# A two-block transformer on one core: an unused strip of 128 bytes in front of the split weights, and a ring of split rows that moves along

## What is computed

```
h @ w  ~  h_hi @ w_hi  +  h_lo @ w_hi  +  h_hi @ w_lo
```

## The kernel before, in words

| rows | distance before | distance after |
|---|---|---|
| HH, HLO, form A and B | 64 bytes | 192 bytes |
| ring HHR, HLR (16 numbers = 64 bytes on) | 0 | 0 |
| LATHI, LATLO (WHI is 73984 and 47104 bytes behind them) | 0 | 128 bytes |

## Time and profile before

### The profile page before, as it was taken

The page is one execution under the profiler, slowest core; times in us unless marked ns, Lnnn a source line. Parts: engine busy times, 40 slices in busy tenths (PEclk is TensorE's granted clock), DMA queues, the critical chain, the costliest instruction groups (busy, mean ns, idle before and its releaser), DMA issues.

```text
span 2110.5 us, 33942 instructions
## 1 busy us (share of the span) xinstructions
PE 2055.3 (97%) x13986; PEld 1863.4 (88%) x13986; DVE 1408.0 (67%) x2157; ACT 1009.3 (48%) x1492; POOL 131.8 (6%) x111
## 2 busy tenths in 40 slices
PE   5999999999999999999999999999999999999997
PEld 1678998788999999998888899999988999999986
DVE  2358999897677677666667576556676755566665
ACT  2234444645454444455445455444565544445553
POOL 0000000013000000000011011000010110000100
PEclk9999999999999999999999999999999999999998
DMA  9998798595777777656655546545555556545553
GB/s 362 383 358 309 240 381 324 197 355 165 236 246 237 233 231 249 196 169 244 190 177 207 176 153 201 197 141 169 164 186 180 174 151 220 168 155 164 177 191 120
DMA packets 267318, 462.98 MB, mean 219 GB/s; under 512 B 21526, under 2 KB 160028, under 8 KB 266652
## 3 DMA queue, kind: packets, MB, share of 16 engines
q1 hardware_dynamic: 265832, 459.66, 64.6%
q10 hardware_dynamic: 1332, 1.14, 0.2%
HBM read 458.62 MB, written 2.13 MB: 218 GB/s over the span
## 4 chain that ended last, share of the span: by engine, by line
PE 84%; DVE 7%; DMA 4%; issue 2%; ACT 2%; ACTq 1%; SPq 0%; POOL 0%; DVEq 0%
PE PS L315 36%; PE PS L314 19%; PE PS L1424 7%; PE PS L1434 7%; PE PS L1426 7%; DVE WLO L305 2%; PE PS L1266 2%; DMA AD<-w_ada 1%; DMA BIG<-w_ada 1%; DVE BIG L391 1%; DVE AD L391 1%; ACT WHI L297 1%; DMA X<-x 1%; PE PS L1280 1%; DVE BIG L1783 1%
## 5 line engine op out<-in xcount | busy, mean ns | idle before, releaser
L305 DVE TENSOR_TENSOR WLO<-RAWT,WHI 128x1024 fp32r<-128x1024 f32 (+7 forms) x694 | 833.0, 1206 | 392.5 <-ACT WHI L297 391.6
L297 ACT ACTIVATE WHI<-RAWT 128x1024 fp32r<-128x1024 f32 (+7 forms) x694 | 694.5, 1015 | 374.0 <-PE PS L1434 205.0
L315 PE MATMUL PS<-WHI,HH 128*128 128x512 f32 (+5 forms) x1296 | 502.6, 388 | 7.4 <-POOL HLO L1114 3.2
L315 PE MATMUL PS<-WHI,HLO 128*128 128x512 f32 (+5 forms) x1296 | 493.6, 381 | 0.0
L315 PE MATMUL PS<-WLO,HH 128*128 128x512 f32 (+5 forms) x1296 | 335.1, 380 | 1.3 <-DVE WLO L305 1.3
L1424 PE MATMUL PS<-HH,WHI 128*128 128x256 f32 x1376 | 325.2, 279 | 0.9 <-ACT HH L1111 0.5
L1426 PE MATMUL PS<-HLO,WHI 128*128 128x256 f32 x1368 | 323.3, 278 | 0.0
L314 PE MATMUL PS<-HH,WHI 128*128 128x256 f32 x1280 | 312.0, 285 | 0.0
L314 PE MATMUL PS<-HLO,WHI 128*128 128x256 f32 x1280 | 303.3, 278 | 0.0
L315 PEld LDWEIGHTS PS<-WHI,HH 128*128 128x128 f32 x1296 | 244.6, 189 | 53.6 <-issue 7.6
L315 PEld LDWEIGHTS PS<-WLO,HH 128*128 128x128 f32 x1296 | 242.7, 188 | 42.2 <-DVE WLO L305 2.3
(11 more groups left out here) (313 smaller groups left out, 1640.5 us busy)
## 6 DMA issues: line engine op xcount, KB each, us to landing
RAWT<-w_in SPq DMA_DIRECT2D x96, 1024.0 KB, 5.2
RAWT<-w_up SPq DMA_DIRECT2D x168, 512.0 KB, 4.9
AD<-w_ada SPq DMA_DIRECT2D x152, 512.0 KB, 6.5
RAWT<-w_out SPq DMA_DIRECT2D x96, 512.0 KB, 4.9
RAWT<-w_down SPq DMA_DIRECT2D x86, 512.0 KB, 4.5
BIG<-w_ada SPq DMA_DIRECT2D x40, 512.0 KB, 12.2
RAWT<-w_in SPq DMA_DIRECT2D x16, 832.0 KB, 4.5
RAWT<-w_in SPq DMA_DIRECT2D x16, 512.0 KB, 4.3
```

Of the source, the lines that this page charges most:

```text
L297: act.activation(WHI[:, (q % HL) * GR:(q % HL) * GR + size], r, ACT.Copy).then_inc(S("hi_done"), 1)
L305: dve.tensor_tensor(WLO[:, (q % HL) * GR:(q % HL) * GR + size], r, h.bitcast(F32), ALU.subtract)\
L315: pe.matmul(o, feat, weight, start=start, stop=stop)
```

## The change

A buffer of 32 numbers, named SHIFT and used by nobody, is allocated between RAWT and WHI. WHI, WLO and all that is allocated behind them (AD, WK, KX, CST, PV, MODC, BADA, SM) lie 128 bytes higher. X, HH, HLO, BIG, LATHI, LATLO and RAWT stay. The ring inside HH and HLO moves by the same 32 numbers. No instruction is added, removed or reordered.

```
         RAWT = sb("RAWT", RAW * 2 * GR)
+        sb("SHIFT", 32)
         WHI, WLO = sb("WHI", HL * GR, F32R), sb("WLO", HL * GR, F32R)
...
-        RING = slice(8 * T + 16, 12 * T + 16)
+        RING = slice(8 * T + 48, 12 * T + 48)
```

## The result

The changed kernel takes 2128.48 us in the median (2127.03 to 2129.81, four runs), the kernel before beside it 2109.41 (four runs): a ratio of 1.0084 [1.0071, 1.0097], 19 us slower. The forecast was 2096; the price of the second rival, the long step everywhere, was 2131. The profiled execution took 2127.03 us.

The account below looks back on a forecast made before the run. TensorE was taken to bound the kernel, with 84% of the chain. Terms 6.9 + 7.0 + 0.5 + 1.4 = 15.8 us less than 2112.3 gave 2096.5, stated as 2096; forecast's own range 2091 to 2104, whole range to 2134.

Parts of the forecast that it names:

- Rival 2: In w_up and block 2's input: the long step everywhere, 21.8 us more (2131), or worse (2148); chance 0.30.
- the long step: The slower matmul duration in w_up and block 2's input, 11.2 ns above the columns' 106.7 ns; expected to go.
- what bounds the kernel: Whole span: TensorE ends last in 84% of the chain, so the time is mostly its steps between matmul starts.
- Rival 1: Whole kernel: nothing moves, since steps depend on something else or the pattern repeats at 128 bytes; 2109 us, chance 0.18.
- 128 bytes count: Operand distances: a 128-byte move acts only if the pattern repeats at more than 128 bytes; otherwise 64 equals 192.
- Why the short step: 256-column matmuls: 0 costs 13.3 ns above the columns, 64 costs 6.7 or 11.2, so 192 should be better.
- form B: Matmuls of 512 columns, some 960 on HH and HLO, distance 64 to 192: taken as 0, bounds 3.1 less, 3.2 more.
- form A: 256-column matmuls on HH and HLO, distance 64 to 192: w_up 6.9, block 2's input 7.0, block 1's 0.5 us less.
- The row with 416 columns: Earlier trace: four matmuls at distance 64 and four at 192 each take 0.75 us, so both distances cost the same.
- latent products: 216 matmuls of 256 columns, distance 0 to 128, from 120.0 ns to 6.7 ns less each: 1.4 us less.
- the ring: Products in w_down and block 2's w_out: it moves with the weights, distance 0 before and after, so nothing changes.
- ScalarE, VectorE, transfers: Copies, subtractions and vector sums on moved addresses: 1.3 us either way, taken as 0; transfers unchanged in count and size.

Follow-up runs that it names:

- experiment 2: Four kernels: the kernel before with WHI and what follows shifted, giving distance 0, 96, 128 or 160 bytes: 2140.74, 2135.02, 2133.46, 2146.57 us.

## Why the prediction was wrong, step by step

- **Right: what bounds the kernel, and that place counts.** The change adds no instruction and no wait, TensorE's clock is the same, its matmul time grew by 18.5 us, and its share of the chain from 84% to 88%. Rival 1, nothing moves, is out: the kernels of experiment 2 differ from that before in addresses alone and take 23 to 37 us more than it. The Trainium skill's page "SBUF — State Buffer", Who interferes with whom, calls TensorE's two read ports independent and says that it never waits on anyone. It speaks of engines against each other; that place is free for TensorE was my reading of it, and these times contradict that reading.
- **Right: 128 bytes count.** 128 bytes matter, and 768, a multiple of 256, do not (tried at one distance, 64). One reading was wrong: the steps of `w_up` do not hold "for over a hundred groups"; the 1723 and 1491 matmuls of the earlier trace rows are 72 and 62 groups of 24.
- **Wrong: "Why the short step".** I ordered the distances 0 and 64 and drew the line on: the cost falls with the distance, so the long step has no hold at 192. Two distances are too few for a trend. The table rises again behind 64, and 160 costs as much as 0. The long stretch at distance 64 was the warning: a cost with two values at one distance is not a function of the distance, and I treated the second value as a remnant that a better place would remove. The sum's terms have the wrong sign for this reason: `w_up` +11.2 us instead of -6.9; block 2 +5.8 with its form B instead of -7.0.
- **Rival 2 was right on `w_up`, and its price is close partly by luck.** It said the long step everywhere, 4730 matmuls that lose 4.6 ns: 21.8 us, 2131; measured 2128.48. The count was too high by the prediction's own rows: their excess over the short step (6.9 + 10.7 + 1.7 = 19.3 us) is that of some 4200 long matmuls, which leaves about 3770 short ones, 17.3 us. The chain shows 11.2 + 4.7 = 15.9 us for form A in `w_up` and block 2; form B (below, 4.2 us by an estimate), which rival 2 did not count, may make up the rest. Its reason, that a load and a stream meet late on this side of a multiple of 256, was tested by no run, and "no short step" is not so: the piece at 1526.31 us has it. In `w_up` alone the stretches of 1727 and 683 matmuls that turned are worth 2410 x 4.6 ns = 11.1 us, and 11.2 were measured. What I held against it, that no row has a long step that L400 can't end, was evidence on one state at one distance; at 192 both L401 groups leave it as it is.
- **Mis-sized: form B of 512 columns.** Taken as 0 by the earlier trace rows, with 3.2 us as the bound. In the x108 piece it costs 234.4 - 230.0 = 4.4 ns more. Over all 960 that would be 4.2 us, an estimate; I did not measure the others one by one. The row with 416 columns did not carry over: its two halves at 64 and 192 cost the same, and the change only swaps them.
- **Mis-sized: latent products.** 120.0 to 118.8 ns, 216 x 1.2 ns = 0.3 us less, not 1.4: distance 128 has a step of its own near 118.5 ns.
- **Right: the ring.** x384 of `w_down` 87.07 us against 87.09. Left in place it cost 9 to 10 us more, which the text named ("from 0 to 128") and did not price.
- **Right: ScalarE, VectorE, transfers.** Nothing of them shows in the time.

**What stays open.** The failed step is shown; the cause beneath it is not. Why a held and a streamed operand at 64 bytes below a multiple of 256 stream in two ways, and why a break of 2, 4 or 8 small matmuls turns the one into the other at this distance where one of 1, 9 or 12 does not, no run here shows. Whether the steps of one kernel differ from execution to execution is open too; executions of the same kernel lie up to 12 us apart, and only one of each was profiled. Seventeen stretches each also say only roughly how often the short step comes.

## What to carry to other kernels

When a kernel is bound by TensorE, divide windows of it by their matmuls before and after any edit of the buffers' layout: here 113.3 against 117.8 ns for one and the same instruction was worth 11 of 19 us in `w_up` alone, and no count or wait showed it. Keep the distance between held and streamed operands below a multiple of 256 bytes fixed when something is put between them, for every pair of buffers, as the ring's move does. Where one instruction has two durations at one setting, find out what turns one into the other before a trend is drawn through either: a small change of a fraction of a per cent may be only that.

## What the runs showed of the hardware

- A matmul's step depends on where its operands lie to each other: 113.2 to 120.0 ns for 256 columns and 226.8 to 235.3 ns for 512 columns, at a granted clock of 1.00. A shift of 768 bytes, three times 256, left the time as it was (ratio 0.9993), one of 128 did not (1.0084).
- The two forms want different places. Form B is cheapest at 0 (228.1 ns, and 226.8 on the ring), where form A has its dearest step, 120.0 (119.8 at 160).
- At distances 64 and 192 the step has two values, 113.3 and 117.8 ns, and at 96 it has 117.3 and 118.5. Each holds for up to 1700 matmuls and turned only where something else stood between. At 64, in single profiled executions, 2, 4 or 8 small matmuls turned it at twelve places of twelve and one at none of five; at 192 one turned it at two of four.
